# Second block's attention: tiles before rotations, the first four mixing tiles from round 20 on, six banks for scores until then

## The chip, the cores and the metric

One core of a Trainium2 chip runs the program in one launch. The metric is the device time of that launch in microseconds, the median of the runs. PE is TensorE (the matrix engine), DVE VectorE, ACT ScalarE, POOL GpSimd, SP the engine that issues the DMAs. PE accumulates into PSUM, which has eight banks; DVE and ACT read it, POOL does not.

## The reference

`reference()` runs two transformer blocks one after the other on x of 256 tokens by 1024 features, in fp32. The first block is not touched by the change. The second block has two layers, and each is

```python
def second_block(x, ...):
    for l in range(DEPTH):                       # DEPTH = 2
        h = rms_norm(x, attn_pre_norm[l])
        mix = hybrid_mixer(h, cos, sin, w_in[l], ..., w_out[l])
        x = x + rms_norm(mix, attn_post_norm[l])
        h = rms_norm(x, ffn_pre_norm[l])
        x = x + rms_norm(conv_ffn(h, ...), ffn_post_norm[l])
```

`hybrid_mixer` projects h by `w_in`, rotates queries and keys (partial_rope), and computes three kinds of attention: "fox" (4 heads, causal, with a forget bias), NSA (8 heads, the sum of three branches with a gate each: compressed, selected, windowed) and dilated (4 heads, a softmax whose terms are weighted by how many patterns hold a key). With 256 tokens the selected and the windowed branch see all causal keys. The compressed branch pools windows of 32 keys and of 32 values through a two-layer net with a tanh gelu:

```python
k_cmp = nsa_compress(kc, ...)                    # gelu(win @ w1) @ w2, 15 windows
p_c, _ = masked_softmax(s_c, cmp_end <= qpos)
o = gb[..., 0:1] * o_c + gb[..., 1:2] * o_s + gb[..., 2:3] * o_w
mix = jnp.concatenate([o_fox, o_nsa, o_dil], axis=-1) @ w_out
```

## The kernel before, in words

The kernel is written for each engine by hand: `tensor`, `scalar`, `vector`, `gpsimd` and `sync` are the five instruction streams, each in its own order. They meet only at semaphores (`wait_ge` on a label that another stream's `then_inc` raises), so an instruction that waits holds up all that stands behind it on its engine.

Weights come in blocks of 128 x 1024 fp32 into a ring of six slots (RING), issued in order by SP; a block's slot is free once PE has used the block six before it. For matmuls of full accuracy a weight block is split: ACT rounds it to the upper part (line 1294, into WH, a ring of four here, up to two blocks ahead of the one PE is at: `ahead`), POOL subtracts it from the block (line 2826, `lowers`) into the lower part RINGL. PE then does three matmuls for each product: upper by upper, upper by the data's rest, lower by upper.

The attention of the second block is `attention2`, once in each of three streams, with the same loop of 28 rounds (`ROUNDS2`). It handles 24 units in pairs: 0 to 3 fox, 4 to 7 dilated, 8 to 15 windowed, 16 to 23 selected. In round i:

- i even, up to 22: `weigh(i)` on PE makes the scores of units i and i+1 in two banks (line 1186); DVE takes the negative maxima (line 2624); ACT the exponentials with their sums (line 1846).
- i odd: DVE's `scale(i-1)` (line 2627) takes the reciprocals of the sums, multiplies them by the branch's gate (windowed and selected units only), and multiplies the weights by the result (one multiplication per half of the queries and unit, four in all). For dilated units it first multiplies by the counts (line 2636).
- `turn_over(i-3)`: PE turns the weights of one unit (line 391), ACT (even units) or DVE (odd ones, line 2658) copies them out.
- i odd: `values(i-5)`: PE multiplies the values by the turned weights of a pair.
- tiles: `TILE_AT` says which of the twelve remaining tiles of `w_in2` is projected in round i (`tile2`, 24 matmuls of 256 columns); the round after, PE rotates it (`rotate2`: one matmul by a permutation, then three DVE instructions by cosine and sine), unless it is tile 11. ACT copies each tile out of PSUM.
- `compress_windows` (DVE, round 9) builds the 15 windows of keys and values; `compress_hidden` (PE, rounds 10 to 13) is the first layer; `compress_fold` (rounds 12 and 14, `FOLD_AT`) sums its four strips, ACT takes the gelu; `compress_out` (round 15) is the second layer; `compressed` (round 16) the scores and, on DVE and ACT, their softmax with the gate; `compressed_over` (round 18) turns the result in four pieces, which ACT copies.
- `MIX_AT` says when a block of `w_mix` (the output projection) is multiplied into the four accumulators (`mix_rows`, 12 matmuls of 512 columns): block 0 in round 14, then 17, 20, 25. Blocks 4 to 7 follow after round 27 in `mix_rest`.

PSUM: `take` (line 366) hands out banks 0 to `in_turn - 1` in turn and waits until the last use of that bank has been read. There are six in turn up to round 9, four in rounds 10 to 13 (banks 4 and 5 hold the hidden sums) and three from round 14 on, since the accumulators of the mixing are banks 3 to 6. Banks 6 and 7 hold the outputs of `values`; from unit 12 on bank 7 alone.

```python
TILE_AT = dict(enumerate((12, 14, 13, 15, 10, 4, 8, 11, 5, 6, 7, 9)))
MIX_AT = {14: 0, 17: 1, 20: 2, 25: 3}
WINDOWS_AT, COMPRESS_AT, SCORES_AT, TURNED_AT = 9, 15, 16, 18
FOLD_AT = {12: 0, 14: 1}
ROUNDS2 = 28
```

Windowed units 8, 10, 12, 14 use query tiles 4, 5, 6, 7 and key tile 10; the selected ones the same queries and key tile 9; the windows are built of tiles 8 and 11; the dilated units use tiles 12 to 15. All matmuls carry line 380, transposes line 391; DVE's helpers `tt` are line 2017, `ts` with one scalar 2021 and with two 2022, ACT's `copy` line 1314.

## Time and profile before

| | |
|---|---|
| median of 3 runs | 2866.33 us (2866.32 to 2869.84) |
| the profiled execution | 2863.9 us |
| its span | 2862.1 us, 42521 instructions |
| PE busy | 2726.0 us (95%) |
| DVE busy | 1330.9 us (47%) |
| ACT busy | 1292.4 us (45%) |
| POOL busy | 1369.5 us (48%) |
| DMA | 361.40 MB, 126 GB/s |
| attention of the second block, layers 0 and 1 | about 2156 to 2281 and 2524 to 2649 |

The profile is of one execution. The times in the trace count from the start of its span. An engine's busy time is that of its instructions; for a matmul the end is modelled. A wait is the idle time of an engine before an instruction, and its releaser the instruction whose semaphore came last. A row of the order in time merges instructions of the same kind that follow each other.

### The profile page before, as it was taken

How to read it: one execution, taken by the hardware profiler on the slowest of the kernel's cores; microseconds unless marked ns; L12 is line 12 of the kernel's file. 1: busy time of each engine (PE TensorE's matmuls, PEld its weight loads, DVE VectorE, ACT ScalarE, POOL GpSimd, SP SyncE). 2: the span in 40 equal slices, each digit the busy share in tenths (PEclk: the TensorE clock that was granted, in tenths of full speed). 3: DMA queues.
4: the chain of work that ended last, by engine and by line, in shares of the span. 5: the costliest groups of instructions: out<-in, count | busy, mean ns of one | idle time of the engine just before them, and what ended most of it. 6: DMA issues, size and time to landing. Idle time of an engine off the chain costs nothing.

```text
span 2862.1 us, 42521 instructions
## 1 busy us (share of the span) xinstructions
PE 2726.0 (95%) x17650; PEld 2315.8 (81%) x17650; DVE 1330.9 (47%) x2614; ACT 1292.4 (45%) x2175; POOL 1369.5 (48%) x616
## 2 busy tenths in 40 slices
PE   7999999999999999998999999989999899998999
PEld 5777877688886787886878879989987599885997
DVE  2778877641333211102768664453126564156541
ACT  3254443423523422223464445654454566554664
POOL 3332021244442544441831428758864278752687
PEclk9999999999999999999999999999999999999999
DMA  6332022132233434333520215535553355543455
GB/s 241 109 124 97 30 74 74 60 121 93 95 126 125 159 123 149 120 96 138 172 83 22 81 61 177 170 106 184 181 193 106 115 157 183 169 138 111 148 183 156
DMA packets 104073, 361.40 MB, mean 126 GB/s; under 512 B 11143, under 2 KB 18567, under 8 KB 103369
## 3 DMA queue, kind: packets, MB, share of 16 engines
q1 hardware_dynamic: 103880, 358.68, 38.6%
q8 instruction: 140, 2.29, 0.3%
q14 instruction: 53, 0.43, 0.1%
HBM read 357.59 MB, written 1.05 MB: 125 GB/s over the span
## 4 chain that ended last, share of the span: by engine, by line
PE 81%; DVE 10%; ACT 5%; DMA 1%; POOL 1%; issue 1%; SPq 0%; DVEq 0%; ACTq 0%
PE PS L380 80%; DVE PS L2025 1%; DVE AR L2017 1%; ACT AR L1314 1%; DMA RING<-w_ada_in 1%; DVE AR L2021 1%; ACT AR L1846 1%; DVE AR L2181 1%; ACT XT L1314 1%; POOL RINGL L2826 1%; DVE AR L2636 1%; DVE SM L2255 1%; ACT WH L1294 1%; ACT L1314 1%; DVE SM L2017 1%
## 5 line engine op out<-in xcount | busy, mean ns | idle before, releaser
L2826 POOL TENSOR_TENSOR RINGL<-RING,WH 128x1024 fp32r<-128x1024 f32 x548 | 1304.3, 2393 | 1424.2 <-ACT WH L1294 1403.7
L1294 ACT ACTIVATE WH<-RING 128x1024 fp32r<-128x1024 f32 x548 | 569.2, 1045 | 687.5 <-PE PS L380 564.7
L380 PE MATMUL PS<-HTR,WH 128*128 128x256 f32 (+2 forms) x2736 | 806.8, 320 | 0.0
L380 PE MATMUL PS<-HTH,WH 128*128 128x256 f32 (+1 forms) x2336 | 683.3, 320 | 4.2 <-POOL HTR L2831 2.5
L380 PEld LDWEIGHTS PS<-HTR,WH 128*128 128x128 f32 (+1 forms) x2736 | 519.6, 190 | 39.8 <-issue 1.8
L380 PEld LDWEIGHTS PS<-HTH,WH 128*128 128x128 f32 x2336 | 443.6, 190 | 42.8 <-issue 11.8
L380 PE MATMUL PS<-ARR,WH 128*128 128x512 f32 (+1 forms) x1856 | 441.9, 341 | 3.5 <-ACT WH L1294 2.6
L380 PE MATMUL PS<-HTH,RINGL 128*128 128x256 f32 (+1 forms) x2336 | 402.7, 315 | 2.3 <-POOL RINGL L2826 2.2
L380 PEld LDWEIGHTS PS<-HTH,RINGL 128*128 128x128 f32 x2336 | 342.2, 191 | 31.1 <-POOL RINGL L2826 3.7
L380 PEld LDWEIGHTS PS<-ARR,WH 128*128 128x128 f32 x1856 | 311.7, 189 | 46.2 <-issue 5.6
L1314 ACT ACTIVATE AR<-PS 128x512 f32<-128x512 f32 (+4 forms) x346 | 163.2, 491 | 315.5 <-PE PS L380 308.8
L2017 DVE TENSOR_TENSOR AR<-AR,PS 128x256 f32<-128x256 f32 (+1 forms) x84 | 45.4, 541 | 464.0 <-PE PS L380 441.0
L380 PE MATMUL PS<-AR 128*128 128x256 f32 (+9 forms) x1016 | 195.8, 372 | 33.2 <-DVE AR L2274 16.3
L380 PE MATMUL PS<-ARR,RINGL 128*128 128x512 f32 (+1 forms) x1120 | 222.3, 341 | 1.7 <-POOL RINGL L2826 1.7
L380 PEld LDWEIGHTS PS<-ARR,RINGL 128*128 128x128 f32 x1120 | 179.1, 189 | 27.0 <-POOL RINGL L2826 2.3
L380 PEld LDWEIGHTS PS<-AR 128*128 128x128 f32 (+4 forms) x1016 | 126.5, 179 | 74.7 <-issue 18.9
L380 PE MATMUL PS<-WH,ARR 128*128 128x512 f32 x544 | 161.4, 392 | 0.0
L2025 DVE SCALAR_TENSOR_TENSOR AR<-PS,CVW,AR 128x255 f32<-128x255 f32 (+1 forms) x176 | 84.5, 482 | 122.2 <-ACT AR L1314 119.1
L2025 DVE SCALAR_TENSOR_TENSOR XT<-XT,AR 128x512 f32<-128x512 f32 (+1 forms) x32 | 39.7, 1253 | 206.5 <-ACT AR L1314 206.5
L380 PEld LDWEIGHTS PS<-WH,ARR 128*128 128x128 f32 x544 | 102.5, 189 | 26.6 <-issue 3.9
L2017 DVE TENSOR_TENSOR AR<-AR 128x256 f32<-128x256 f32 (+1 forms) x158 | 94.4, 616 | 51.9 <-ACT AR L1314 50.0
L2025 DVE SCALAR_TENSOR_TENSOR PS<-Z,CVW,PS 128x482 f32<-128x482 f32 (+9 forms) x150 | 110.8, 739 | 4.9
(217 smaller groups left out, 3304.0 us busy)
## 6 DMA issues: line engine op xcount, KB each, us to landing
RING<-w_ada_in SPq DMA_DIRECT2D x96, 512.0 KB, 3.6
RING<-w_up_in SPq DMA_DIRECT2D x88, 512.0 KB, 3.5
RING<-w_gates_in SPq DMA_DIRECT2D x48, 512.0 KB, 3.4
RING<-w_ff_gate_in SPq DMA_DIRECT2D x44, 512.0 KB, 3.9
RING<-w_ff_up_in SPq DMA_DIRECT2D x44, 512.0 KB, 3.5
RING<-w_down_in SPq DMA_DIRECT2D x44, 512.0 KB, 3.5
...
```

The source lines that it names most:

```text
L380: return e.matmul(out_, lhsT, rhs, start=start, stop=stop)
L1294: e.activation(RINGS[name][:, j, 0:width], RING[:, b % NSLOT, 0:width], ACT.Copy).then_inc(*a_upper.up(b))
L1314: return e.activation(out_, in_, f, bias=bias, scale=scale)
L1846: t = e.activation(PQ[u % 6][:, w], ps("w2", l, u)[:, w], ACT.Exp, bias=NMX[:, u, qt:qt + 1], accum_out=DN[:, u, qt:qt + 1])
L2017: return e.tensor_tensor(out_, a, b, op)
L2021: return e.tensor_scalar(out_, a, s1, None, op0)
L2025: return e.scalar_tensor_tensor(out=out_, in0=a, scalar=s, in1=b, op0=op0, op1=op1)
L2181: e.copy_predicated(dst, LM[:, i, :].bitcast(I32), src).then_inc(*d_gla.up("pred", l, u, i))
L2255: e.tensor_reduce(MXC[:, c], ps("score", l, who, u)[:, 0:n], AXX, ALU.max).then_inc(*d_att.up("rmax", l, who, u))
L2636: t = e.scalar_tensor_tensor(out=pq[:, w], in0=pq[:, w], scalar=1.0, in1=CNT[:, w], op0=ALU.mult, op1=ALU.mult, accum_out=DN[:, n, qt:qt + 1])
L2826: e.tensor_tensor(RINGL[:, i, 0:width], RING[:, i, 0:width], RINGS[name][:, j, 0:width], ALU.subtract).then_inc(*g_lower.up(b))
```

## The change

PE's order within a round becomes: scores, this round's tile, rotation of the last round's tile. Tile 5 is projected in round 6, and 8 and 11 a round later each. The two folds become one in round 14, into one bank, with one gelu on ACT. The mixing blocks 0 to 3 go to rounds 20, 22, 24 and 26; the banks in turn are six from round 14 on and three from round 20 on. ACT rounds the first mixing block in round 18. DVE's softmax of the compressed scores is cut in two: the first part goes to the end of its round 16, the rest (`compressed_weights`) to the end of round 17, ACT's exponential to round 17, the turning to round 19. The branch gate is no longer multiplied into the reciprocals; each multiplication of the weights has the gate's column as a second scalar. The eight gate products of the compressed branch become one.

```diff
@@ -264,6 +264,7 @@
         XW = AR[:, 8192:9216].rearrange("p (a k n) -> p a k n", a=2, k=16)
         HIDP = AR[:, 5632:6144].rearrange("p (a n) -> p a n", a=2)
         HID = AR[:, 9424:9544].rearrange("p (a j n) -> p a j n", a=2, j=2)
+        HIDS = AR[:, 9424:9544].rearrange("p (m n) -> p m n", m=4)
         KCMP = AR[:, 9984:10016]
         VC = AR[0:15, 9296:9424]
         W2 = AR[:, 9600:9984].rearrange("p (j n) -> p j n", j=2)
@@ -301,8 +302,8 @@
         ROTATED = {4, 5, 6, 7, 8, 9, 10, 12, 13, 14, 15}
         QUERIES = {q for _, _, q, *_ in UNITS}
         FIRST_TILES = (0, 2, 1, 3)
-        TILE_AT = dict(enumerate((12, 14, 13, 15, 10, 4, 8, 11, 5, 6, 7, 9)))
-        MIX_AT = {14: 0, 17: 1, 20: 2, 25: 3}
+        TILE_AT = dict(enumerate((12, 14, 13, 15, 10, 4, 5, 8, 11, 6, 7, 9)))
+        MIX_AT = {20: 0, 22: 1, 24: 2, 26: 3}
         MIX_ROWS = (0, 1, 6, 7, 2, 3, 4, 5)
         XTOK = [[XT[:, 4 * t + 2 * h:4 * t + 2 * h + 2, 256:512] for h in range(2)] for t in range(2)]
         XU = [[XT[:, 4 * t + 2 * h:4 * t + 2 * h + 2, 0:256] for h in range(2)] for t in range(2)]
@@ -325,9 +326,8 @@
         def mixed(l, name, t, h):
 
             return p_block.to(name, l) if (t, h) == (1, 1) else p_mix.to("mixed", l, name, t, h)
-        WINDOWS_AT, COMPRESS_AT, SCORES_AT, TURNED_AT = 9, 15, 16, 18
+        WINDOWS_AT, FOLD_AT, COMPRESS_AT, SCORES_AT, TURNED_AT = 9, 14, 15, 16, 19
         HIDDEN_AT = {10: (0, 0), 11: (0, 1), 12: (1, 0), 13: (1, 1)}
-        FOLD_AT = {12: 0, 14: 1}
         ROUNDS2 = 28
 
         def mix_bank(u):
@@ -1139,16 +1139,18 @@
                     t.then_inc(*p_block.up(n))
                 p_block.also("hidden", l, a)
 
-            def compress_fold(l, a):
-                o = take("hid", l, a, until=(a_mix, "hid", l, a))
-                pe.wait_ge(*a_mix.to("hidp", l, a))
-                for j in range(2):
-                    t = mm(o[:, 32 * j:32 * j + 30], HIDP[:, a, 128 * j:128 * j + 128], FOLD, True, True)
-                t.then_inc(*p_mix.up("hid", l, a))
+            def compress_fold(l):
+                o = take("hid", l, until=(a_mix, "hid", l))
+                pe.wait_ge(*a_mix.to("hidp", l, 1))
+                for a in range(2):
+                    for j in range(2):
+                        t = mm(o[:, 64 * a + 32 * j:64 * a + 32 * j + 30], HIDP[:, a, 128 * j:128 * j + 128], FOLD,
+                               True, True)
+                t.then_inc(*p_mix.up("hid", l))
 
             def compress_out(l):
                 o = take("kcmp", l, until=(a_mix, "kcmp", l))[:, 0:30]
-                pe.wait_ge(*a_mix.to("hid", l, 1))
+                pe.wait_ge(*a_mix.to("hid", l))
                 pe.wait_ge(*w2_in.to(l))
                 for j in range(2):
                     t = mm(o, W2[:, j, 0:128], HID[:, 0, j, :], j == 0, j == 1)
@@ -1233,16 +1235,16 @@
 
                 in_turn[0] = 6
                 for i in range(ROUNDS2):
-                    if i in (10, 14):
-                        turn[0], in_turn[0] = 0, {10: 4, 14: 3}[i]
+                    if i in (10, 14, 20):
+                        turn[0], in_turn[0] = 0, {10: 4, 14: 6, 20: 3}[i]
                     if i < 24 and i % 2 == 0:
                         weigh(i)
+                    if i in TILE_AT:
+                        tile2(l, TILE_AT[i], h)
                     if i - 1 in TILE_AT and TILE_AT[i - 1] in ROTATED:
                         rotate2(l, TILE_AT[i - 1])
-                    if i in TILE_AT:
-                        tile2(l, TILE_AT[i], h)
-                    if i in FOLD_AT:
-                        compress_fold(l, FOLD_AT[i])
+                    if i == FOLD_AT:
+                        compress_fold(l)
                     if i in HIDDEN_AT:
                         compress_hidden(l, *HIDDEN_AT[i])
                     if i == COMPRESS_AT:
@@ -1812,10 +1814,10 @@
                 act.wait_ge(*p_block.to("hidden", l, a))
                 copy(HIDP[:, a, :], ps("hidden", l, a)[:, 0:256]).then_inc(*a_mix.up("hidp", l, a))
 
-            def compress_hidden(l, a):
-                act.wait_ge(*p_mix.to("hid", l, a))
-                copy(HID[:, a], ps("hid", l, a)[:, 0:64].rearrange("p (j n) -> p j n", j=2)[:, :, 0:30],
-                     ACT.Gelu_apprx_tanh).then_inc(*a_mix.up("hid", l, a))
+            def compress_hidden(l):
+                act.wait_ge(*p_mix.to("hid", l))
+                copy(HIDS, ps("hid", l)[:, 0:128].rearrange("p (m n) -> p m n", m=4)[:, :, 0:30],
+                     ACT.Gelu_apprx_tanh).then_inc(*a_mix.up("hid", l))
 
             def compress_out(l):
                 act.wait_ge(*p_mix.to("kcmp", l))
@@ -1876,15 +1878,15 @@
                         weigh(i + 1)
                     if i in TILE_AT:
                         tile2(l, TILE_AT[i])
-                    if i in FOLD_AT:
-                        compress_hidden(l, FOLD_AT[i])
-                    if i == 12:
+                    if i == FOLD_AT:
+                        compress_hidden(l)
+                    if i == 18:
                         uppers(stage_block["w_mix", l, 0])
                     if i in HIDDEN_AT and HIDDEN_AT[i][1]:
                         compress_sums(l, HIDDEN_AT[i][0])
                     if i == COMPRESS_AT:
                         compress_out(l)
-                    if i == SCORES_AT:
+                    if i == SCORES_AT + 1:
                         compressed(l)
                     if i == TURNED_AT:
                         compressed_over(l)
@@ -2594,11 +2596,16 @@
                     dve.wait_ge(*p_mix.to("cscore", l))
                     e.tensor_copy(pc, src).then_inc(*d_mix.up("pc", l, par))
                 flat = PC.rearrange("p u q n -> p (u q) n")
-                fm, fd, fr = (x.rearrange("p u q -> p (u q)") for x in (m, d, r))
+                fm = m.rearrange("p u q -> p (u q)")
                 dve.wait_ge(*d_mix.to("pc", l, 1))
                 e.tensor_reduce(fm, flat, AXX, ALU.max).then_inc(*d_mix.up("pcm", l))
                 dve.wait_ge(*d_mix.to("pcm", l))
                 tt(flat, flat, bc(fm, 2, 15), ALU.subtract).then_inc(*d_mix.up("pcs", l))
+
+            def compressed_weights(l):
+                m, d, r = CM_
+                flat = PC.rearrange("p u q n -> p (u q) n")
+                fd, fr = (x.rearrange("p u q -> p (u q)") for x in (d, r))
                 dve.wait_ge(*a_mix.to("pce", l))
                 tt(PC, PC, bc(C01, 1, 8), ALU.mult).then_inc(*d_mix.up("pc01", l))
                 dve.wait_ge(*d_mix.to("pc01", l))
@@ -2609,10 +2616,9 @@
                 e.reciprocal(fr, fd).then_inc(*d_mix.up("pcr", l))
                 dve.wait_ge(*d_mix.to("pcr", l))
                 dve.wait_ge(*a_mix.to("gq", l, 1))
-                for u in range(8):
-                    h = 4 * (u % 2) + u // 2
-                    t = tt(r[:, u, :], r[:, u, :], GQ[:, :, 3 * h], ALU.mult)
-                t.then_inc(*d_mix.up("pcg", l))
+                gate = GQ.rearrange("p t (par i br) -> p i par t br", par=2, i=4)[:, :, :, :, 0]
+                r4 = r.rearrange("p (i par) q -> p i par q", par=2)
+                tt(r4, r4, gate, ALU.mult).then_inc(*d_mix.up("pcg", l))
                 dve.wait_ge(*d_mix.to("pcg", l))
                 tt(flat, flat, bc(fr, 2, 15), ALU.mult).then_inc(*d_mix.up("pcw", l))
 
@@ -2639,15 +2645,15 @@
                     if kind == "dil":
                         dve.wait_ge(*d_mix.to("counted", l, u + 1))
                     e.reciprocal(rc, dn).then_inc(*d_mix.up("rec", l, u))
-                    if br is not None:
-                        dve.wait_ge(*d_mix.to("rec", l, u))
-                        gate = GQ.rearrange("p t (par m) -> p par t m", par=2)[:, :, :, 3 * (o - 2) + br]
-                        tt(rc, rc, gate, ALU.mult).then_inc(*d_mix.up("rec", l, u))
                     dve.wait_ge(*d_mix.to("rec", l, u))
                     for n in (u, u + 1):
                         pq = PQ[n % 6]
                         for qt, w in HALVES:
-                            t = ts(pq[:, w], pq[:, w], RC[:, n, qt:qt + 1], None, ALU.mult)
+                            if br is None:
+                                t = ts(pq[:, w], pq[:, w], RC[:, n, qt:qt + 1], None, ALU.mult)
+                            else:
+                                g = 12 * (n - u) + 3 * (o - 2) + br
+                                t = ts(pq[:, w], pq[:, w], RC[:, n, qt:qt + 1], GQ[:, qt, g:g + 1], ALU.mult, ALU.mult)
                         t.then_inc(*d_mix.up("weighed", l, n))
 
                 def turn_over(u):
@@ -2681,14 +2687,16 @@
                         rotate2(l, TILE_AT[i - 1])
                     if i == WINDOWS_AT:
                         compress_windows(l)
-                    if i == SCORES_AT:
-                        compressed(l)
                     if 0 <= i - 3 < 24:
                         turn_over(i - 3)
                     if 0 <= i - 4 < 24:
                         values(i - 4)
                     if 0 <= i - 5 < 24:
                         lower(i - 5)
+                    if i == SCORES_AT:
+                        compressed(l)
+                    if i == SCORES_AT + 1:
+                        compressed_weights(l)
 
             def mix_out(l, name, nid, gain):
 
```

## Rows read from the trace of the kernel before

**Rows 1.** Page, section 4: the chain that ended last, by engine.

```profile
PE 81%; DVE 10%; ACT 5%; DMA 1%; POOL 1%; issue 1%; SPq 0%; DVEq 0%; ACTq 0%
```

**Rows 2.** Windows: busy PE, PEld, DVE, ACT, POOL; granted clock; DMA.

```profile
2156.00:2281.00 125.00, 108.68 (x807) 82.04 (x806) 82.68 (x223) 59.76 (x166) 40.02 (x17) 0.97 0.32 106
2524.00:2649.00 125.00, 108.95 (x816) 82.38 (x816) 83.20 (x224) 61.42 (x168) 41.17 (x18) 0.99 0.32 107
...
2177.00:2218.00 41.00, 35.69 (x285) 29.42 (x283) 35.23 (x90) 16.91 (x50) 15.25 (x7) 1.00 0.30 94
```

**Rows 3.** Waits of PE in 2156 to 2281: total us, times, longest.

```profile
PE PS L380 <- ACT AR L1314: 7.5, 8, 2.0
```

**Rows 4.** PE in time: start, us, operation, count, idle before and releaser.

```profile
2178.86 0.47 PE L380 MATMUL PS<-HTH,WH 128*128 128x256 f32 x1
...
2181.91 0.49 PE L391 MATMUL PS<-CM,AR 128*128 128x128 f32 x3
...
2204.97 0.67 PE L380 MATMUL PS<-AR,CM 128*128 128x256 f32 x2 [1.97 <-ACT AR L1314]
...
2211.35 0.50 PE L380 MATMUL PS<-Z 128*128 128x384 bf16 x2 [1.70 <-DVE AR L2017]
...
2216.16 1.07 PE L380 MATMUL PS<-RING,AR 128*32 128x256 f32 x16
...
2231.76 0.50 PE L380 MATMUL PS<-Z 128*128 128x384 bf16 x2 [1.11 <-ACT AR L1314]
...
2238.18 1.15 PE L380 MATMUL PS<-AR 128*128 128x30 f32 x12 [1.35 <-ACT AR L1314]
...
2244.10 0.70 PE L380 MATMUL PS<-WH,ZR 128*128 128x512 f32 x2
...
2246.93 0.49 PE L391 MATMUL PS<-CM,AR 128*128 128x128 f32 x3
2250.67 1.20 PE L380 MATMUL PS<-AR 128*64 128x256 f32 x8 [3.24 <-DVE AR L2658]
...
2269.64 0.55 PE L391 MATMUL PS<-CM,AR 128*128 128x128 f32 x3 [1.95 <-ACT AR L1846]
...
2280.13 0.73 PE L380 MATMUL PS<-WH,ZR 128*128 128x512 f32 x2
```

**Rows 5.** DVE in order of time, same columns.

```profile
2205.68 1.37 DVE L2017 TENSOR_TENSOR SM<-SM,AR 128x4 f32<-128x4 f32 x1
2207.08 3.09 DVE L2021 TENSOR_SCALAR AR<-AR,SM 128x128 f32<-128x128 f32 x4
...
2219.51 0.17 DVE L2017 TENSOR_TENSOR SM<-SM,AR 128x4 f32<-128x4 f32 x1
...
2247.22 2.48 DVE L2017 TENSOR_TENSOR SM<-SM,AR 128x2 f32<-128x2 f32 x8
```

**Rows 6.** POOL in order of time, same columns.

```profile
2204.63 4.73 POOL L2826 TENSOR_TENSOR RINGL<-RING,WH 128x1024 fp32r<-128x1024 f32 x2 [6.53 <-ACT WH L1294]
```

**Rows 7.** DVE groups by form from 1900: busy us, mean ns, idle before.

```profile
L2021 DVE TENSOR_SCALAR AR<-AR,SM 128x256 f32<-128x256 f32 x48 | 16.7, 347 | 0.0
...
L2017 DVE TENSOR_TENSOR SM<-SM,AR 128x4 f32<-128x4 f32 x16 | 11.2, 700 | 0.5
```

**Rows 8.** Line 2022: duration ns min/median/max, first and last start.

```profile
L2022 DVE TENSOR_SCALAR HT<-HT,MOD x32: 404/414/1385, 45.0 to 1917.2; 128x256 f32<-128x256 f32 x32
```

**Rows 9.** The chain in time, 2196 to 2219: start us, us, what.

```profile
2201.33 0.54 DVE SM L2624 x2
...
2201.89 1.72 ACT AR L1846 x8
2203.61 0.94 ACT WH L1294
```

**Rows 10.** ACT in order of time, same columns.

```profile
2236.57 1.28 ACT L1314 ACT_TABLE_LOAD   x1
2237.86 0.22 ACT L1314 ACTIVATE AR<-PS 128x60 f32<-128x60 f32 x1
```

## The prediction

> **What bounds the kernel now.** I read the page's chain first: PE is 81% of it, DVE 10%, ACT 5% [rows 1]. The change touches only the attention of the second block, which stands twice in the trace (2156 to 2281 and 2524 to 2649), so I read those stretches next. There PE is busy 108.7 of 125 us, about 0.87, and DVE 82.7 [rows 2]; the second layer repeats the first with nearly the same sums. So at most some 16 us of idle PE stand in a layer, and a little more is lost to the clock: a mean of 0.97 and 0.99 over 125 us is 3.8 and 1.3 us of PE work lost [rows 2], 2.5 on average. Between 2177 and 2218 DVE is busy 35.2 of 41 us [rows 2]: in this half of the stretch PE does not wait for itself. The list of waits says "ACT", 7.5 us in eight pieces [rows 3], yet ACT there had been waiting for DVE's maxima. The order in time shows the pieces that count [rows 4]: 1.97 before a rotation, 1.70 before weigh(10), 1.11 before weigh(14), 1.35 before the compressed projections, 3.24 before values(12), 1.95 before a transpose in round 23.
>
> What slows DVE is seen by holding its rows against POOL's. A gate product of four elements takes 1.37 us at 2205.68, and 0.17 at 2219.51, where POOL is idle [rows 5]; the four multiplications behind the slow one take 3.09 and end 0.8 us behind POOL's pair of subtractions, which runs from 2204.63 to 2209.36 [rows 6]. So a DVE instruction that meets a POOL subtraction waits for its end, and POOL issues them in pairs.
>
> **The gates.** The 16 products of 128x4 are 11.2 us busy, 0.70 each [rows 7], against 0.17 where nothing meets them. It would be wrong to book 11.2. At 2205.68 the product is stalled to the end of the first subtraction, and the four multiplications behind it are stalled in their turn, 3.09 us at 2207.08 [rows 5], to the end of the pair at 2209.36 [rows 6]. Without the product, the first multiplication takes that stall. I book 8 x 0.20 (0.17 and a gap) = 1.6 us of DVE per layer. Against it the 32 multiplications get a second column. A multiplication by two columns, 256 wide, takes 414 ns [rows 8], one by a single column 347 [rows 7]: 32 x 0.067 = 2.1 us. Net +0.5 us of DVE per layer, ends 0 and +2.1, since they are on the chain only where DVE is. A two-column one also reaches 1385 ns [rows 8], so it is stalled too.
>
> The eight gate products of the compressed branch end 0.5 us after the subtraction that held the first (2.48 at 2247.22 [rows 5]); as one they save about 0.5.
>
> **Rounds 0 to 10.** Each rotation now goes behind the next tile, 3.05 us of PE (2178.86 to 2181.91 [rows 4]), and tile 5 comes two rounds earlier. PE's waits for ACT's copy go, and so do the 1.97 and 1.70: these and the shorter ones before them make some 6 us. But DVE gets each rotation later. Behind weigh(2) come DVE's first maxima (0.54), ACT's exponentials (1.72) and the rounding of the next weights (0.94) [rows 9], then POOL's pair: 3.5 us after PE's weigh, with 0.3 for the handovers. The rotation arrives a tile and itself later, 3.05 + 0.35, and the first of its products that reads two tiles in memory follows 0.4 behind, at 3.8: lost by a quarter of a microsecond. Its two such products then wait for one subtraction of the pair each (4.73 us [rows 6]); the rotated keys are ready when PE has been at weigh(4) for 1.7 us, and DVE's next maxima are a microsecond late. DVE stays full from there on. The walk brings compress_windows out 1.4 us later than before; PE, which no longer waits at rotations, is there 6 us early, and waits in one piece before hidden(0, 0) (2216.16 before [rows 4]). So the 6 us are not won, they are moved. As the race is close I take half of 1.4: **+0.7** (ends -6, all idle gone, and +5, one more pair of 4.73 met), and **+1.3** for one half-speed stretch after the long idle, half of the mean of 2.5 rounded (ends 0 and 3.8).
>
> **Rounds 10 to 13.** They are PE's own. The rotation no longer stands before the tile (0.8 with its wait), one fold and its reading go to round 14 (0.6), and the wait of 1.11 before weigh(14) [rows 4] goes, because the first Gelu with its table load of 1.28 [rows 10] and the loads back are off ACT before that copy: **-2.5** (ends -3 and 0).
>
> **Rounds 14 to 27.** Before: 2231.76 to 2280.13, 48.4 us [rows 4], four mixing tiles of 2.83 in it (2244.10 to 2246.93). Idle are 1.35 + 3.24 + 1.95 and small ones of 1.3, with the clock 10.3. The 3.24 goes: DVE now copies the turned tile of round 13 before it starts on the compressed softmax, and does not sit out ACT's exponential. But what stood under the chain scores, exponentials, table load, Gelu, projections were the first two mixing tiles, 5.7 us; they now stand behind round 20. Without them I walk: 2.9 idle in round 15 (exponentials end 2.4 us after weigh(14), then 1.28 and 0.3, less 1.3 of PE work), 2.4 before the turned compressed weights in round 19, 0.7 more for the exponentials of 18 and 19, which queue behind compressed_weights on DVE, 2.2 before weigh(20), whose bank is freed only by ACT's last copy of those weights, behind a rounding. Six banks do not help here, since it is data that is late. From round 20 the mixing tiles fill the 1.95 and the small ones, 0.3 stay. With the second fold (0.5) and one slow stretch (1.3) that makes 10.3: **0** (ends -5, where the slow stretches and half the new idle stay out, and +4, three slow stretches and POOL's six subtractions now met by DVE in rounds 20 to 27).
>
> The Gelu switch is where a page differs. The row shows the load at 2236.57 for 1.28 us, and the activation starts 0.01 us behind its end [rows 10]. The Trainium skill, "ScalarE: Activation LUTs", What ACT_TABLE_LOAD costs, puts a drain of 1.38 us on top, 2.66 in all. By it, round 15 would wait 1.4 us longer in each layer and the whole come out 2.8 us later; the row decides.
>
> DMA issues do not change in number or size. Blocks of w_in2, w_cmp and w_mix change places in SP's queue of six; the first mixing blocks are in the ring from about round 14 and held there, and nothing behind them is wanted before they are consumed, so I cost that at nothing (if a slot came late, it would show as ACT's rounding waiting). POOL and ACT do the same subtractions and roundings. The mixing rest after round 27 stays as it is.
>
> **Sum.** Per layer +0.7 + 1.3 - 2.5 + 0 = -0.5, both -1.0. The profiled execution is 2863.9 us (span 2862.1 and 1.8 around it), 2.4 under the median of the runs shown, 2866.33; so 2862.9 for such an execution and 2865.3 as a median.
>
> **Rivals.** *The idle is really won.* If the rotations reach DVE before POOL's pairs, DVE is not late at round 10: -3 there, no slow stretch, -2.5, and -2 of rounds 14 to 27 because two of the 1.3 stay out; -7.5 per layer, 2851. For it: six of PE's waits are removed by name, and the race is lost by only 0.25 us. Against: DVE's 35.2 of 41.
>
> *DVE falls a pair behind.* In rounds 2 to 9 the rotation is met by both subtractions and the scaling, which follows it, by the next; one more of 4.73 per layer before compress_windows, less 1 of slack: +4 on +0.7, with -1 from a slow stretch that is then hidden: +3.5 in all, so +7, 2873. It decides when the second product of a rotation starts after POOL's subtraction in every pair of rounds.
>
> *The clock.* The Trainium skill, "TensorE: Matmul & The Clock Gate", HAM oscillation, warns that idle gaps between bursts bring the lower rate back. As a mechanism here: 6, 2.9, 2.4 and 2.2 us of idle each followed by half speed, four times 1.3 where I have two: +2.6 per layer, 2870.5. The trace bears out that much: the 3.24 idle stands in a stretch whose granted clock is 0.97 instead of 1.00, that is 2.4 GHz with pieces at 1.2.
>
> **Chances.** About 0.2%, 5.7 us, is what a measurement of this kernel can tell from no change. Forecast (within it): 0.38, own range 2860.6 to 2872.1. Idle won, whole or half: 0.36, faster. DVE a pair behind 0.16 and the clock's beyond the bound 0.10: 0.26, slower. The ends of the parts reach much further, but the parts do not all go one way; 2851 to 2877 leaves out one in five.
>
> **What would show it.** Right: in the changed profile PE's idle of 1.97 and 1.70 is gone and 4 to 6 us stand before the first hidden products; values(12) has no wait over 0.5; idle of 2 to 3 us before the compressed projections, the turned weights and weigh(20); PE's busy sum nearly unchanged; two-column multiplications of 0.35 and 0.41 us; two table loads fewer per layer. Wrong: hidden(0, 0) before 2213, or rounds 14 to 27 under 45 us.

## The result and the profile after

The changed kernel takes 2876.32 us (median of 6 runs, 2870.65 to 2880.92) against 2867.47 for the kernel before in the same comparison (6 runs, 2864.62 to 2870.87): the ratio is 1.0040, 95% interval 1.0028 to 1.0052. It is slower, by twice the 0.2% that a measurement can tell. The plain quotient of the two medians is smaller, 1.0031, so the loss is 9 to 11.5 us. The forecast was no change.

| | before | after |
|---|---|---|
| profiled execution | 2863.9 us | 2877.65 us |
| its span | 2862.1 us | 2875.9 us |
| PE busy | 2726.0 us | 2738.5 us |

The two profiled executions lie 13.75 us apart, more than the medians (8.85). What follows splits the distance between these two executions.

From the page of the changed kernel, sections 1 (busy us, share of the span, instructions) and 4 (the chain); the second line answers to [rows 1]:

```profile
PE 2738.5 (95%) x17650; PEld 2322.8 (81%) x17650; DVE 1338.8 (47%) x2584; ACT 1287.1 (45%) x2169; POOL 1370.2 (48%) x616
...
PE 81%; DVE 11%; ACT 5%; DMA 1%; POOL 1%; issue 1%; SPq 0%; DVEq 0%; ACTq 0%
```

The shares of the chain are nearly unchanged and tell nothing. The first line does: the program has the same matmuls, yet PE is busy for 12.5 us more. To see where, I cut each attention at scores(0), scores(14) and the start of the mixing rest, in both kernels. The columns of the windows are those of [rows 2]: length, busy PE, PEld, DVE, ACT, POOL, granted clock, DMA share and GB/s. Rounds 14 to 27 of the kernel before (its rounds 0 to 13 take 75.14 and 75.12 us, at 1.00):

```profile
2231.76:2280.13 48.37, 40.36 (x259) 26.81 (x259) 27.30 (x85) 25.28 (x70) 13.18 (x6) 0.93 0.21 70
...
2600.02:2646.49 46.47, 38.71 (x260) 25.50 (x260) 27.29 (x85) 25.30 (x70) 13.16 (x6) 0.96 0.21 73
```

The kernel after, with the same three cuts (these answer to [rows 2]):

```profile
2156.55:2230.65 74.10, 67.17 (x536) 53.75 (x534) 55.04 (x139) 31.50 (x92) 25.15 (x11) 0.95 0.40 127
2230.65:2284.68 54.03, 43.98 (x265) 28.80 (x263) 30.38 (x69) 24.85 (x70) 14.38 (x6) 0.87 0.19 64
2531.01:2605.52 74.51, 67.68 (x535) 54.19 (x534) 54.99 (x139) 31.50 (x92) 25.46 (x11) 0.95 0.40 127
2605.52:2660.24 54.72, 44.72 (x266) 29.59 (x264) 30.49 (x69) 24.85 (x70) 14.37 (x6) 0.84 0.19 62
```

Rounds 0 to 13 got shorter by 1.04 us in layer 0 and by 0.61 in layer 1. Rounds 14 to 27 got longer, 48.37 to 54.03 and 46.47 to 54.72, by 5.66 and 8.25. Together, with what rounds 0 to 13 won, that is 12.3. Another 1.6 lies between the two attentions: the 32 transposes behind the mixing rest took 5.46 us where they took 3.92 before, in a stretch with a granted clock of 0.97 for 1.00 (from them to scores(0) of layer 1: 227.67 before, 229.24 after).

The same rows split the 5.66 and 8.25. Length less PE's busy time is its idle time: 8.01 and 7.76 before, 10.05 and 10.00 after, so +2.0 and +2.2. The rest, +3.6 and +6.0, is PE's busy time. About 0.5 us of it in each layer is moved work: the first fold now stands here and not in round 12 (one fold takes 0.46 us before, both take 0.92 after). What is left, 3.2 and 5.5, goes with the granted clock, which fell from 0.93 and 0.96 to 0.87 and 0.84. So by PE's busy time some 60% of the loss in these rounds is clock and 30% idle.

PE's waits in the attention of layer 0 (total us, times, longest), which answer to [rows 3]:

```profile
PE PS L380 <- DVE AR L2019: 5.2, 2, 5.0
PE PS L380 <- ACT AR L1316: 4.6, 2, 2.7
...
PE PS L391 <- DVE AR L2024: 1.9, 1, 1.9
```

And PE in order of time, columns as in [rows 4], to which these answer:

```profile
2177.24 0.48 PE L380 MATMUL PS<-Z 128*128 128x384 bf16 x2 [1.64 <-DVE SM L2647]
...
2215.94 1.94 PE L380 MATMUL PS<-RING,AR 128*32 128x256 f32 x16 [4.96 <-DVE AR L2019]
...
2236.05 1.18 PE L380 MATMUL PS<-AR 128*128 128x30 f32 x12 [2.67 <-ACT AR L1316]
...
2244.40 0.87 PE L380 MATMUL PS<-AR 128*64 128x256 f32 x8 [0.41 <-DVE AR L2664]
...
2248.94 2.00 PE L391 MATMUL PS<-CM,AR 128*15 128x128 f32 x16 [1.91 <-DVE AR L2019]
...
2254.43 0.80 PE L380 MATMUL PS<-Z 128*128 128x384 bf16 x2 [1.94 <-ACT AR L1316]
...
2256.74 1.22 PE L380 MATMUL PS<-WH,ZR 128*128 128x512 f32 x2
...
2263.54 0.74 PE L380 MATMUL PS<-WH,ZR 128*128 128x512 f32 x2
...
2274.67 0.70 PE L391 MATMUL PS<-CM,AR 128*128 128x128 f32 x3 [1.93 <-DVE AR L2024]
...
2278.10 1.22 PE L380 MATMUL PS<-WH,ZR 128*128 128x512 f32 x2
```

What the reader is to see: the 1.97 before a rotation and the 1.70 before scores(10) of [rows 4] are gone, and one piece of 4.96 stands before the first hidden product, with a new one of 1.64 before scores(4). The 3.24 before values(12) has become 0.41. In their place stand 2.67 before the compressed projections, 1.91 before the turned compressed weights, 1.94 before scores(20), and 1.93 before the transposes of round 25. The durations tell the rest: the row of two mixing matmuls takes 1.22 us at 2256.74 and again at 2278.10, and 0.74 at 2263.54. The first 16 hidden products take 1.94 us, where the same row took 1.07 before [rows 4].

The windows of the changed kernel behind the five long idles show that this is the clock (columns as above; the clock is the third number from the end):

```profile
2213.50:2220.30 6.80, 4.36 (x28) 3.10 (x29) 6.01 (x22) 2.27 (x10) 0.00 (x0) 0.50 0.30 99
2237.40:2240.80 3.40, 3.40 (x19) 1.74 (x19) 0.00 (x0) 1.96 (x4) 0.00 (x0) 0.50 0.00 0
2248.90:2251.10 2.20, 2.00 (x16) 1.38 (x16) 1.42 (x5) 1.74 (x9) 0.00 (x0) 1.00 0.04 7
2254.45:2257.85 3.40, 3.40 (x13) 1.94 (x14) 1.24 (x5) 0.46 (x3) 0.07 (x1) 0.50 0.00 0
2274.95:2281.75 6.80, 6.59 (x24) 3.96 (x23) 1.89 (x5) 2.16 (x4) 2.37 (x1) 0.50 0.04 16
```

Behind 4.96, 2.67, 1.94 and 1.93 us of idle PE runs at 0.50, the 1.2 GHz level, for 3.4 or 6.8 us (the first of these begins 2.4 us before the idle ends); behind the 1.91 (2248.90) it does not. These are four such stretches in layer 0's attention. The kernel before had a clock of 1.00 in rounds 0 to 13, and behind them 0.93 and 0.96.

### The profile page after: what moved, and what is told of

Same layout as the page of the kernel before. It is cut to its first block, busy times and chain, and to the rows that moved or that the text cites. A ratio compares the mean times of both kernels' runs of the same rounds, so it can differ in the third digit from the quotient of the medians.

```text
span 2875.9 us, 42484 instructions
## 1 busy us (share of the span) xinstructions
PE 2738.5 (95%) x17650; PEld 2322.8 (81%) x17650; DVE 1338.8 (47%) x2584; ACT 1287.1 (45%) x2169; POOL 1370.2 (48%) x616
## 4 chain that ended last, share of the span: by engine, by line
PE 81%; DVE 11%; ACT 5%; DMA 1%; POOL 1%; issue 1%; SPq 0%; DVEq 0%; ACTq 0%
PE PS L380 80%; DVE AR L2019 2%; DVE PS L2027 1%; ACT AR L1316 1%; DMA RING<-w_ada_in 1%; DVE AR L2024 1%; DVE AR L2183 1%; ACT XT L1316 1%; POOL RINGL L2834 1%; DVE AR L2023 1%; ACT WH L1296 1%; DVE SM L2257 1%; ACT AR L1848 1%; POOL HTR L2839 1%; DVE AR L2642 1%
## 5 line engine op out<-in xcount | busy, mean ns | idle before, releaser
L380 PEld LDWEIGHTS PS<-ARR,WH 128*128 128x128 f32 x1856 | 311.6, 189 | 47.7 <-issue 7.4
L1316 ACT ACTIVATE AR<-PS 128x512 f32<-128x512 f32 (+6 forms) x344 | 163.4, 494 | 292.4 <-PE PS L380 288.9
```

Source lines behind the costliest of these rows:

```text
L380: return e.matmul(out_, lhsT, rhs, start=start, stop=stop)
L1316: return e.activation(out_, in_, f, bias=bias, scale=scale)
```

## The experiments

Twelve kernels ran, in three groups, each beside runs of the kernel before on the same chip. The medians of before were 2862.85 (29 runs), 2866.90 (14) and 2864.84 (35) in the three, so kernels of different groups are compared by their ratios. The changed kernel itself was not run again beside them; its ratio is that of the section above. In the table, us are of the one profiled execution, layer 0 / layer 1; idle and clock (the granted one) are of rounds 14 to 27.

| kernel | ratio, 95% interval | rounds 0-13 | rounds 14-27 | idle | clock |
|---|---|---|---|---|---|
| before | 1 | 75.1 / 75.1 | 48.4 / 46.5 | 8.0 / 7.8 | 0.93 / 0.96 |
| after | 1.0040 (1.0028-1.0052) | 74.1 / 74.5 | 54.0 / 54.7 | 10.1 / 10.0 | 0.87 / 0.84 |
| mixing back | 0.9979 (0.9970-0.9988) | 74.9 / 74.8 | 43.0 / 44.2 | 5.6 / 5.5 | 1.00 / 0.96 |
| mixing alone | 1.0047 (1.0031-1.0064) | 74.2 / 74.2 | 53.7 / 56.3 | 10.8 / 12.2 | 0.87 / 0.85 |
| order back | 1.0025 (1.0015-1.0035) | 73.6 / 73.5 | 52.2 / 53.8 | 9.2 / 9.7 | 0.87 / 0.87 |
| gates back | 1.0029 (1.0020-1.0038) | 74.1 / 74.5 | 54.1 / 52.3 | 10.1 / 9.4 | 0.87 / 0.87 |
| filling, too much | 1.0029 (1.0018-1.0040) | 75.6 / 76.9 | 52.9 / 53.0 | 1.7 / 1.7 | 1.00 / 1.00 |
| mixing, order back | 0.9965 (0.9952-0.9978) | 73.6 / 73.5 | 44.4 / 47.7 | 5.5 / 5.7 | 0.96 / 0.89 |
| mixing, gates back | 0.9969 (0.9957-0.9981) | 75.9 / 75.0 | 45.5 / 45.7 | 5.0 / 5.6 | 0.93 / 0.93 |
| all three back | 0.9964 (0.9951-0.9977) | 73.6 / 74.1 | 44.4 / 44.5 | 5.6 / 5.6 | 0.96 / 0.96 |
| filling, half | 0.9995 (0.9986-1.0003) | 73.1 / 73.1 | 48.6 / 48.6 | 3.5 / 3.5 | 1.00 / 1.00 |
| three back, filling | 0.9989 (0.9980-0.9997) | 73.6 / 73.6 | 49.6 / 48.2 | 5.6 / 5.6 | 0.90 / 0.93 |
| two tiles back | 0.9988 (0.9978-0.9998) | 75.0 / 74.7 | 46.1 / 45.9 | 6.9 / 6.7 | 0.96 / 0.96 |
| softmax alone | 0.9990 (0.9981-0.9999) | 75.2 / 75.1 | 48.3 / 45.2 | 6.7 / 6.7 | 0.89 / 0.96 |

### Mixing back: the changed kernel with its mixing tiles, banks and first rounding as before

```diff
-        MIX_AT = {20: 0, 22: 1, 24: 2, 26: 3}
+        MIX_AT = {14: 0, 17: 1, 20: 2, 25: 3}
...
-                    if i in (10, 14, 20):
-                        turn[0], in_turn[0] = 0, {10: 4, 14: 6, 20: 3}[i]
+                    if i in (10, 14):
+                        turn[0], in_turn[0] = 0, {10: 4, 14: 3}[i]
...
-                    if i == 18:
+                    if i == 12:
                         uppers(stage_block["w_mix", l, 0])
```

> The changed kernel with the mixing tiles back in rounds 14, 17, 20 and 25, three banks in turn from round 14 and the rounding of the first one in ACT's round 12; all else stays changed. Cover theory (the first two mixing tiles kept PE busy under the compressed branch in rounds 14 to 19; without them PE stands idle there and its clock falls to the lower level): from scores(14) to the mixing rest the traces show 48.4 and 46.5 us before, 54.0 and 54.7 after, so 13.9 us come from there; this kernel gives them back, 2860 to 2866 us, at or under the kernel before. Order theory (the rotations behind the tiles starve DVE, and the 5 us before the first hidden products bring the clock down): nearly nothing comes back, 2873 to 2877.

Measured: 2857.63 us (12 runs), 0.9979, as the cover theory said. Undoing the move turns the slower kernel into one faster than before. The step is 17 us from 1.0040 to 0.9979, and 14 by the plain quotients of medians (1.0031 and 0.9982). The place of the tiles, the number of banks in turn and the first rounding went back together, here and in every version below that moves them, so they are not told apart. Rounds 14 to 27 of this kernel, windows:

```profile
2231.00:2274.05 43.05, 37.40 (x263) 25.53 (x263) 26.58 (x72) 23.96 (x69) 13.27 (x6) 1.00 0.25 82
2595.22:2639.39 44.17, 38.66 (x264) 26.26 (x264) 26.63 (x72) 24.30 (x69) 13.28 (x6) 0.96 0.25 82
```

43.05 us where the changed kernel took 54.03. In layer 0 the granted clock is 1.00, so 37.40 is what PE's work of these rounds takes at full rate. That gives the price of the clock in the others: 43.98 less 37.40 is 6.6 us in the changed kernel's layer 0, and 7.3 in layer 1. The kernel before has one fold less in these rounds, 36.94 at full rate, so its price is 3.4 and 1.8. The rest of the 11 us between the changed kernel and this one is idle, 5.6 against 10.05. PE in time:

```profile
2237.39 1.15 PE L380 MATMUL PS<-AR 128*128 128x30 f32 x12 [0.87 <-ACT AR L1316]
...
2251.82 0.61 PE L391 MATMUL PS<-CM,AR 128*15 128x128 f32 x4 [2.61 <-DVE AR L2664]
...
2265.17 0.55 PE L391 MATMUL PS<-CM,AR 128*128 128x128 f32 x3 [1.84 <-ACT AR L1848]
```

The first mixing tile now ends just ahead of the compressed projections: 0.87 idle where the changed kernel has 2.67. The 2.61 before the turned weights is longer than the changed kernel's 1.91, and the 1.84 in round 23 nearly as long as its 1.94 and 1.93, but no half speed stands behind them in this layer.

### Mixing alone: the kernel before with only that part of the change

The same three edits in the other direction, on the kernel before.

> The kernel before with only the mixing tiles (rounds 20, 22, 24, 26), the six banks from round 14 and three from round 20, and the first rounding in ACT's round 18 changed. Cover theory: slower than before by 10 to 15 us, since the waits under the softmax (3.24 us in round 17) and the Gelu stay and nothing covers them. Order theory: within 3 us of before.

Measured: 2877.30 us (6 runs), 1.0047, within the 10 to 15 us of the cover theory. It alone is as slow as the whole change. PE in time:

```profile
2235.28 1.18 PE L380 MATMUL PS<-AR 128*128 128x30 f32 x12 [3.07 <-ACT AR L1314]
...
2247.48 1.55 PE L380 MATMUL PS<-AR 128*64 128x256 f32 x8 [4.27 <-DVE SM L2641]
```

Both waits of the kernel before that the tiles had partly covered (1.35 and 3.24 in [rows 4]) grew, to 3.07 and 4.27, by 1.7 and 1.0.

### Order back: the changed kernel with rotations ahead of tiles

```diff
-        TILE_AT = dict(enumerate((12, 14, 13, 15, 10, 4, 5, 8, 11, 6, 7, 9)))
+        TILE_AT = dict(enumerate((12, 14, 13, 15, 10, 4, 8, 11, 5, 6, 7, 9)))
...
-                    if i in TILE_AT:
-                        tile2(l, TILE_AT[i], h)
                     if i - 1 in TILE_AT and TILE_AT[i - 1] in ROTATED:
                         rotate2(l, TILE_AT[i - 1])
+                    if i in TILE_AT:
+                        tile2(l, TILE_AT[i], h)
```

> The changed kernel with each rotation ahead of the tile again and the tiles in their old order. Cover theory: 2872 to 2878, since only the waits up to round 13 move, which came out 1 us per layer better after than before. Order theory: the clock stays up in round 10, 6 to 8 us come back, 2868 to 2870.

Measured: 2871.06 us (12 runs), 1.0025. Rounds 0 to 13 take 73.6 and 73.5, less than the 74.1 and 74.5 with the new order, and with a clock of 1.00 instead of 0.95. In these profiles the new order does not win in its own rounds. The front's idle over 0.15 us sums to 6.9 in the changed kernel's layer 0 and to 7.1 here: it is moved, most of it into one piece, and the one piece is followed by half speed. As times of the whole kernel the two do not differ clearly: the intervals of 1.0025 and 1.0040 overlap, and the plain quotients of medians are 1.0029 and 1.0031.

### Gates back: the changed kernel with the gate in the reciprocals

```diff
+                    if br is not None:
+                        dve.wait_ge(*d_mix.to("rec", l, u))
+                        gate = GQ.rearrange("p t (par m) -> p par t m", par=2)[:, :, :, 3 * (o - 2) + br]
+                        tt(rc, rc, gate, ALU.mult).then_inc(*d_mix.up("rec", l, u))
...
-                            if br is None:
-                                t = ts(pq[:, w], pq[:, w], RC[:, n, qt:qt + 1], None, ALU.mult)
-                            else:
-                                g = 12 * (n - u) + 3 * (o - 2) + br
-                                t = ts(pq[:, w], pq[:, w], RC[:, n, qt:qt + 1], GQ[:, qt, g:g + 1], ALU.mult, ALU.mult)
+                            t = ts(pq[:, w], pq[:, w], RC[:, n, qt:qt + 1], None, ALU.mult)
```

> The changed kernel with the branch gate multiplied into the reciprocals again, one scalar in each multiplication. Cover and order theory: within 2 us of the changed kernel. Gate theory (a two-column multiplication is 0.067 us longer, 32 per layer, all on the chain): 4 us faster than the changed kernel, 2872.

Measured: 2872.03 us (12 runs), 1.0029; the interval overlaps that of the changed kernel. Layer 0 is the same to 0.1 us in both halves. Layer 1 is 2.4 shorter in rounds 14 to 27: 1.7 less of PE's busy time, as much as 3.4 us at half speed cost, and 0.65 less idle. The gate's own price is too small to be told from that; neither the 4 us of the gate theory nor nothing is excluded.

### Mixing with order, mixing with gates, and all three as before

Each is the first experiment with the third, the fourth, or both added. The last leaves of the change the softmax in two parts with its later turning, the single fold with its single gelu, and the single gate product of the compressed branch.

> The changed kernel with the mixing tiles and the order of tiles and rotations as before; the softmax in two parts, one fold and the two-column gates stay. If the rotations behind the tiles cost 4 us also here, as they did with the mixing tiles moved (1.0025 against 1.004), this is 2853 to 2855 us; if that cost came from the coincidence with the moved tiles, it is within 2 us of the kernel with the mixing tiles alone back (0.9979).

> The changed kernel with the mixing tiles as before and the gates in the reciprocals as before. Two-column multiplications measured 334 and 401 ns for 128 and 256 columns against 281 and 347 for one column; if that is on the chain, 3 us faster than with the mixing tiles alone back, 0.9968; if DVE has slack with the mixing tiles back, within 1.5 us.

> The changed kernel with mixing tiles, order and gates as before: what is left of the change is the softmax in two parts behind DVE's copy, the single fold with one gelu, the one gate product of the compressed branch and the later turning. Cover theory: the wait of 3.24 us in round 17 and two table loads per layer go with nothing lost, 8 to 12 us faster than before, 0.996 to 0.997. If the gains of the change sit in the order instead, no faster than 0.999.

Measured: 2857.15 (6 runs), 2857.85 (5 runs) and 2855.84 us (5 runs); 0.9965, 0.9969, 0.9964. Once the mixing is back, the intervals of all four kernels overlap: what order and gates add, 4 and 3 us by the expectations or nothing, is too small to be told. The last is the fastest kernel of the study by its ratio, 0.36% or 10 us under the kernel before, as the cover theory had it. Its rounds 14 to 27, windows:

```profile
2233.42:2277.82 44.40, 38.79 (x265) 26.38 (x263) 26.40 (x78) 24.48 (x69) 13.21 (x6) 0.96 0.25 85
2598.25:2642.80 44.55, 38.91 (x263) 26.42 (x263) 26.42 (x78) 24.31 (x69) 13.21 (x6) 0.96 0.24 81
```

Against the kernel before these are 4.0 and 1.9 us shorter. Its waits in PE's order of time:

```profile
2208.16 0.67 PE L380 MATMUL PS<-AR,CM 128*128 128x256 f32 x2 [1.98 <-ACT AR L1316]
...
2254.28 3.84 PE L391 MATMUL PS<-CM,AR 128*15 128x128 f32 x19 [2.56 <-DVE AR L2664]
...
2268.91 0.55 PE L391 MATMUL PS<-CM,AR 128*128 128x128 f32 x3 [1.96 <-ACT AR L1848]
```

### Softmax alone: the kernel before with one part

```diff
-        WINDOWS_AT, COMPRESS_AT, SCORES_AT, TURNED_AT = 9, 15, 16, 18
+        WINDOWS_AT, COMPRESS_AT, SCORES_AT, TURNED_AT = 9, 15, 16, 19
```

with DVE's `compressed` cut in two and ACT's exponential a round later, as the change has them.

> The kernel before with one edit: DVE's compressed softmax in two parts behind its copies, ACT's exponential and the turning a round later. If the 3.24 us wait before values(12) and the half speed behind it were what the good part of the change wins, nearly all of the 11 us of the version with three edits undone comes from here: 2856 to 2860. If the single fold with its single table load and gelu carries a share, 2860 to 2864.

Measured: 2860.37 us (11 runs), 0.9990. Idle in rounds 14 to 27 falls by 1.3 and 1.1 us, rounds 0 to 13 stay at 75.1. The 3.24 before values(12) is gone, but 3.0 stand before the turned weights: most of the wait has moved. The expectation that nearly all of the gain comes from here failed: the intervals of 0.9990 and 0.9964 do not touch. The other one, that the single fold carries a share, fits, but no run tells the fold from the single gate product. With the single fold and product on top, the version with all three back, the front is 1.5 and 1.0 shorter and idle behind another 1.1.

### Two tiles back: where the mixing tiles count

The changed kernel with tiles 0 and 1 in rounds 14 and 17, tiles 2 and 3 in 22 and 26, and the banks and first rounding of the first experiment.

```diff
-        MIX_AT = {20: 0, 22: 1, 24: 2, 26: 3}
+        MIX_AT = {14: 0, 17: 1, 22: 2, 26: 3}
```

> The changed kernel with its first two mixing tiles back in rounds 14 and 17, the third and fourth in 22 and 26 as late as the change has them, three banks for scores from round 14 on. If what costs is that nothing stands under the chain of scores, exponentials, gelu and projections in rounds 14 to 19, this is within 3 us of the version with all four tiles back: 2858 to 2861. If what costs is POOL's subtractions of the last tiles meeting DVE in rounds 20 to 27, half or more of the loss stays: 2866 to 2873.

Measured: 2859.62 us (12 runs), 0.9988. Rounds 14 to 27 take 46.1 and 45.9: 7.9 and 8.9 under the changed kernel, 3.1 and 1.7 over the version with all four back. So most of the loss is the two tiles that stood under the chain scores, exponentials, gelu and projections, as the first theory said, and a smaller part is the last two. PE in time:

```profile
2249.55 0.61 PE L391 MATMUL PS<-CM,AR 128*15 128x128 f32 x4 [2.60 <-DVE AR L2664]
...
2266.06 0.55 PE L391 MATMUL PS<-CM,AR 128*128 128x128 f32 x3 [1.45 <-DVE AR L2024]
```

The small part, 3.1 us in layer 0, is 1.2 of idle and 1.9 of PE's busy time, at a clock of 0.96. In it stands the 1.45 before the transposes of round 25, and that wait is for DVE. In the changed kernel the same wait is 1.93 (the row at 2274.67 above). DVE and POOL in time, of the changed kernel; first DVE (it answers to [rows 5]):

```profile
2261.33 4.33 DVE L2024 TENSOR_SCALAR AR<-AR,SM 128x128 f32<-128x128 f32 x4
...
2269.56 2.43 DVE L2019 TENSOR_TENSOR ARR<-AR,ZR 128x256 fp32r<-128x256 f32 x1 [2.04 <-ACT ZR L1316]
...
2272.12 3.08 DVE L2024 TENSOR_SCALAR AR<-AR,SM 128x128 f32<-128x128 f32 x4
```

then POOL (answering to [rows 6]):

```profile
2260.24 4.69 POOL L2834 TENSOR_TENSOR RINGL<-RING,WH 128x1024 fp32r<-128x1024 f32 x2 [5.72 <-ACT WH L1296]
2269.30 4.91 POOL L2834 TENSOR_TENSOR RINGL<-RING,WH 128x1024 fp32r<-128x1024 f32 x2 [4.37 <-ACT WH L1296]
```

The pair of subtractions of a late mixing block runs from 2269.30 to 2274.21. DVE's one tensor instruction of 256 columns at 2269.56 takes 2.43 us (0.42 at 2276.01 with POOL idle), and the four multiplications behind it, which the transposes wait for, 3.08. That is the same stall as before, now met in rounds 20 to 27, as the forecast's upper end had it. Not every DVE instruction is stalled so: under POOL's pair from 2205.68 to 2210.41 a product with one operand in PSUM took 0.42 us at 2206.19 and a reciprocal 0.17 at 2206.53, as long as without POOL, and only the four multiplications behind them were late (4.41).

### The filling: the clock by itself

`hum(n)`, which the kernel already has for other places, multiplies a constant by a constant n times into a bank, once the last use of that bank has been read; nobody reads the result.

```diff
+                    if i == 10:
+                        hum(38, 4)
                     if i in HIDDEN_AT:
                         compress_hidden(l, *HIDDEN_AT[i])
                     if i == COMPRESS_AT:
+                        hum(20)
                         compress_out(l)
...
                     if i == TURNED_AT:
+                        hum(14)
                         compressed_over(l)
```

and in the same way 16 before scores(20) and 14 before the transposes of round 25.

> The changed kernel with matmuls of constants added on PE in the five places where its trace shows PE idle: 38 before the first hidden products (4.96 us idle there), 20 before the compressed projections (2.67), 14 before the turned compressed weights (1.91), 16 before scores(20) (1.94) and 14 before the transposes of round 25 (1.93). They compute nothing that is used, and each is about 0.06 us at the full clock. Clock theory (of the 13.7 us lost about half is matmuls at half speed behind these idle pieces, 47.8 us at the lower level in the two attentions and behind them against 13.7 before): faster than the changed kernel by 5 to 9 us although work is added, granted clock 1.00 nearly throughout the attention. Idle theory (only the waits cost): no faster, or slower by up to 3 us.

Measured: 2874.79 us (9 runs), 1.0029. Each product cost 0.228 us, nearly four times the 0.06 taken, so the fillings were longer than the idles (8.64 us in the idle of 4.96): none of the five idles is left, the clock is 1.00 throughout, and rounds 14 to 27 take 52.9 and 53.0. It could not tell the theories apart: what the clock gave back the filling took, and the interval overlaps that of the changed kernel. The second filling had half as many (19, 10, 7, 7, 7).

> The changed kernel with constant matmuls, about half as many as in the first filling: by 0.228 us each 4.3 us before the first hidden products, 2.3 before the compressed projections, 1.6 each before the turned compressed weights, before scores(20) and before round 25's transposes. All are shorter than the idle they stand in (4.96, 2.67, 1.91, 1.94, 1.93), so they cost PE nothing by themselves. If the half-speed stretches are the loss (20.5 and 23.9 us at the lower level per layer, half of which is lost work), at most a quarter of them is left and the time falls by 10 us or more, to 2866 or less. If the data are late whatever the clock does, the filled places only wait again later: under 4 us, 2872 to 2876, with the lower level gone from the records all the same.

Measured: 2861.75 us (11 runs), 0.9995, against 1.0040 for the same kernel without filling (in another comparison); the intervals do not touch. The step is 12 to 13 us. Windows:

```profile
2154.44:2227.56 73.12, 69.76 (x574) 56.90 (x572) 55.08 (x139) 31.47 (x92) 25.11 (x11) 1.00 0.40 130
2227.56:2276.18 48.62, 45.09 (x328) 32.86 (x326) 30.91 (x69) 24.82 (x70) 14.41 (x6) 1.00 0.21 70
2522.46:2595.58 73.12, 69.69 (x573) 56.89 (x571) 55.12 (x139) 31.46 (x92) 25.48 (x11) 1.00 0.41 130
2595.58:2644.21 48.63, 45.10 (x327) 32.85 (x326) 30.93 (x69) 24.82 (x70) 14.43 (x6) 1.00 0.21 70
```

The clock is 1.00 in all four, and each half takes the same time in both layers, to 0.01 us. Against the changed kernel 1.0 and 1.4 us are won in rounds 0 to 13, 5.4 and 6.1 in rounds 14 to 27. PE in time:

```profile
2208.66 4.40 PE L380 MATMUL PS<-CM 128*128 128x128 f32 x38
2213.82 1.07 PE L380 MATMUL PS<-RING,AR 128*32 128x256 f32 x16 [0.75 <-DVE AR L2027]
...
2247.79 1.83 PE L380 MATMUL PS<-CM 128*128 128x128 f32 x14
2249.80 0.48 PE L380 MATMUL PS<-Z 128*128 128x384 bf16 x2 [0.18 <-ACT AR L1324]
...
2251.07 0.73 PE L380 MATMUL PS<-WH,ZR 128*128 128x512 f32 x2
```

The fillings (PS<-CM, x38 and x14) lie where the idle was and leave 0.75 and 0.18 of it. The 16 hidden products take 1.07 us again and the first two mixing matmuls 0.73. The first hidden product comes no earlier, 59.4 us behind scores(0) in both; the work behind it is faster. In rounds 14 to 27 of layer 0 the 31 constant products are 7.1 us of the 45.09 busy; the other work takes 38.0 instead of 43.98. Of these 6.0 us 0.6 come back as idle (3.5 and the 7.1 are 10.6, against 10.05), so 5.4 are won. Nothing but the fillings was changed, so this shows what the half speed cost: 6.4 us in layer 0 and 7.5 in layer 1. The 48.62 that are left at full clock, against 43.05 of the version with mixing back, are the price of the idle, 5.6.

### Three back with a filling: a miss

The version with all three back, and nine `hum` before the turned compressed weights.

> The kernel before with only the softmax in two parts, the single fold and the single gate product (the three other edits undone), and nine constant matmuls, 2.05 us, in the 2.56 us that PE idles before the turned compressed weights. Clock theory: the 3.4 us at half speed behind that idle go in both layers, 1.7 us per layer, 2852 to 2854 against 2855.8 without the filling. Rival, the stretch behind it is bound by DVE and ACT: no difference (2855 to 2857).

Measured: 2861.11 us (11 runs), 0.9989; worse than without it (0.9964). PE in time:

```profile
2248.43 3.83 PE L380 MATMUL PS<-CM 128*128 128x128 f32 x18 [2.60 <-ACT AR L1849]
```

With three banks in turn the filling itself waits 2.60 us for a bank that ACT's exponentials are still reading, and then runs where the transposes would, at half speed at that (3.83 us for 18 records). It came on top: from scores(14) to scores(20) 27.57 us against 25.43. It neither shortened an idle nor kept the clock (0.90 and 0.93), so it says nothing for or against either theory. A filling has to have a bank that nobody holds. The fillings in the changed kernel had: no row of theirs shows a wait before it.

## Why the prediction was wrong

**Rounds 0 to 13 came out near, in part by luck.** Forecast -0.5 per layer, measured -1.04 and -0.61. By parts, in layer 0: from scores(0) to the first hidden product -0.15 where +0.7 was taken (the waits of 1.97 and 1.70 gone, 4.96 in one piece, the first hidden product at 2215.94 against 2216.16); the half-speed stretch behind it 1.0 and 1.4 by the half filling, forecast 1.3; what is left, about -1.9, against -2.5. The 0.9 taken too much in the first part and the 0.6 in the last offset each other. In the last, the fold and the wait of 1.11 brought their 1.6 (rounds 0 to 13 of the version with order back), and the rotation's 0.8 only about 0.3. So "the 6 us are not won, they are moved" holds, and the rival by which the idle is really won, with nearly as great a chance as the forecast, is out for this reason.

**Rounds 14 to 27 are the step that failed**, in the term of one slow stretch (1.3) and in the idle behind round 20 (0.3). The forecast set 10.3 us of idle, fold and clock against 10.3: **0**. Measured is +5.66 and +8.25. By its terms:

- *Idle.* Forecast 8.5 (2.9 + 2.4 + 0.7 + 2.2 + 0.3) and 0.5 for the fold. Measured 10.05. The places were right: 2.67 for 2.9, 1.91 for 2.4, 1.94 for 2.2. Left out was round 25, where 0.3 was taken for everything behind round 20 and 1.93 came, by POOL's pairs, which stood in the upper end as "POOL's six subtractions now met by DVE" and were not in the value.
- *Clock.* Forecast one slow stretch of 1.3. Measured 6.6 and 7.3 us of PE's busy time, against 3.4 and 1.8 before; 5.4 and 6.1 by the half filling. This is the large term. I had put down one stretch in a part where my own list had three idles of over 2 us. And a stretch costs more than the 1.3 taken from the mean of 0.97 and 0.99 over 125 us: where PE is busy throughout, 3.4 us at 0.50 cost 1.7, and 6.8 cost 3.4.
- *What was won.* "The 3.24 goes" held (0.41 is left). But the version with mixing back shows what the same edits bring with the tiles where they were: 43.05 us at full rate in layer 0, 5.3 under the kernel before. The tiles' move added 4.4 of idle and 6.6 of busy time at the lower clock to that. The expected gain was there and was given back by the move, twice over.

**The signs.** All but one of those listed came: the idles of 1.97 and 1.70 gone, 4.96 before the first hidden products, 0.41 before values(12), idle where it was named (two of the three just under 2 us). The one that failed is "PE's busy sum nearly unchanged". It rose by 12.5, and that is the clock that the sum left out.

**The rivals.** The clock is what happened: I named the mechanism and the places, and gave it a chance of 0.10 and too small a price. Its four stretches of 1.3 make 5.2 us per layer, where the half filling gives 6.4 and 7.5, and it put the whole 4.2 us over the kernel before, where the medians are 8.85 apart and the two profiled attentions 12.3. Against the kernel before, measured is +4.6 and +7.6 per layer. Clock makes 3.2 + 1.0 and 5.5 + 1.4 of it; the new idle is 2.0 and 2.2 and the fold that moved in 0.5, against which rounds 0 to 13 won 2.0 apart from the clock. The rule of the Trainium skill, "TensorE: Matmul & The Clock Gate", HAM oscillation, that idle gaps between bursts of work bring the lower rate back, is borne out by the trace: granted clock 0.50 behind four idles of 1.93 to 4.96 us, though not behind the fifth, of 1.91. *DVE a pair behind* did not come in the front, where the first hidden product is no later; in the back its mechanism is the 1.93 of round 25. Its sum was also wrong: +4, and -1 for a slow stretch, on the forecast's -0.5 make +2.5 per layer, 2871, and not +3.5 and 2873.

**The gates.** A two-column multiplication was put at 414 ns for 256 columns, with one column 347. Line 2024 (duration ns min/median/max) shows it:

```profile
L2024 DVE TENSOR_SCALAR AR<-AR,SM x64: 334/402/2502, 2206.7 to 2650.5; 128x128 f32<-128x128 f32 x32, 128x256 f32<-128x256 f32 x32
```

The shortest takes 334 ns, the median is 402, in line with the 350 and 410 expected of the two widths; the longest is 2502. The tiny gate products' stall went over to the multiplications, as said: at one and the same place in the front the product and the four multiplications took 1.37 + 3.09 us before [rows 5], and the four alone 4.41 at 2206.73 after. DVE's busy time in rounds 14 to 27 rose from 27.30 to 30.38 us, but not by the gates: with the gates back it is 30.29, with the mixing moved alone 31.83, with the mixing back 26.58. It is the moved tiles, whose subtractions meet the multiplications. The gates' net price in time stays within the measurement's uncertainty.

**The Gelu switch.** ACT in time, which answers to [rows 10]:

```profile
2234.43 1.28 ACT L1316 ACT_TABLE_LOAD   x1
2235.72 0.27 ACT L1316 ACTIVATE AR<-PS 128x120 f32<-128x120 f32 x1
```

The load takes 1.28 us and the activation starts 0.01 behind its end, so the row was right and the drain of 1.38 us that the Trainium skill, "ScalarE: Activation LUTs", What ACT_TABLE_LOAD costs, adds is not seen here either. The idle there came out 0.2 under my walk, not 1.4 over. Loads in the two attentions fell from 14 to 10, two fewer per layer as expected.

**The range.** 2876.32 lies outside the forecast's own 2860.6 to 2872.1 and inside the wide 2851 to 2877, at its very end: that it is inside owes to the width, not to the sum. Slower was given 0.26.
